# Second norm of three block boundaries from three sums gathered early, odd residual tiles on GpSimd

## What is computed

```python
def rmsnorm(x, g):
    xf = x.astype(jnp.float32)
    y = xf * lax.rsqrt(jnp.mean(xf * xf, axis=-1, keepdims=True) + EPS)
    return (y * g.astype(jnp.float32)).astype(x.dtype)
...
        f = swiglu(rmsnorm(h, ffn1_pre_g[l]), ffn1_w_gate[l], ffn1_w_up[l], ffn1_w_down[l])
        h = h + 0.5 * rmsnorm(f, ffn1_post_g[l])
        m = hybrid_mixer(rmsnorm(h, mix_pre_g[l]), w_in[l], b_gate[l], q_norm_g[l], w_uq[l],
                         kv_norm_g[l], w_ukv[l], w_sb_o[l], w_mla_o[l], w_out[l])
        h = h + rmsnorm(m, mix_post_g[l])
        f = swiglu(rmsnorm(h, ffn2_pre_g[l]), ffn2_w_gate[l], ffn2_w_up[l], ffn2_w_down[l])
        h = h + 0.5 * rmsnorm(f, ffn2_post_g[l])
    return h[:, N_META:]
...
        h = rms_norm(x, norm1_g[l]) * (1.0 + sc1) + sh1
        z = h @ w_in[l]
```

## Time and profile before

| | |
|---|---|
| median of 3 runs | 1902.59 us (1902.04 to 1903.81) |
| the profiled execution's own time | 1902.07 us |
| its span | 1900.3 us |
| mean granted PE clock | 0.986 of full speed |

### The profile page before, as it was taken

How to read it: one execution, slowest core, us unless ns; L and a number is a source line. 1 busy time by engine, 2 the same in 40 slices (tenths; PEclk the granted TensorE clock), 3 DMA queues, 4 the chain that set the end, 5 groups by cost and what they waited for, 6 DMA issues and landing times.

```text
span 1900.3 us, 30514 instructions
## 1 busy us (share of the span) xinstructions
PE 1804.4 (95%) x11032; PEld 1143.7 (60%) x11033; DVE 1024.9 (54%) x1509; ACT 524.7 (28%) x847; POOL 852.6 (45%) x481
## 2 busy tenths in 40 slices
PE   8999998998999999998999999999989999999987
PEld 7999896677899998888633333333333333333332
DVE  6776642345687575658455554454454554444444
ACT  5333443635643345345310110110110110011011
POOL 0000000000000026647178777777777777777774
PEclk9999999989999999899999999999999999999999
DMA  9777452213476643333899999999999999999995
GB/s 350 262 257 262 175 178 89 67 48 111 164 270 251 202 156 136 132 112 133 354 373 419 416 419 416 418 418 417 419 417 408 417 417 418 417 419 417 419 417 221
DMA packets 98894, 560.96 MB, mean 295 GB/s; under 512 B 9008, under 2 KB 11184, under 8 KB 50480
## 3 DMA queue, kind: packets, MB, share of 16 engines
q1 hardware_dynamic: 98688, 560.02, 74.9%
q10 hardware_dynamic: 144, 0.07, 0.0%
HBM read 559.00 MB, written 1.05 MB: 295 GB/s over the span
## 4 chain that ended last, share of the span: by engine, by line
PE 70%; DMA 15%; DVE 7%; ACT 3%; POOL 3%; issue 2%; SPq 0%; POOLq 0%; DVEq 0%; ACTq 0%
PE bank L1193 16%; DMA stage<-w_exp_in 15%; PE bank L665 12%; PE bank L667 11%; PE bank L666 11%; PE bank L1280 8%; POOL ring L1720 2%; DVE cst L1745 2%; PE bank L1204 1%; PE bank L646 1%; PE bank L908 1%; DVE cst L2288 1%; DVE arena L1745 1%; DVE cst L1749 1%; PE bank L1260 1%
## 5 line engine op out<-in xcount | busy, mean ns | idle before, releaser
L1720 POOL COPY ring<-stage 128x2048 f32<-128x2048 f32 x372 | 717.7, 1937 | 249.4 <-DMA stage<-w_exp_in 134.9
L1193 PE MATMUL bank<-ring,arena 128*64 128x512 f32 x2112 | 474.9, 597 | 11.2 <-POOL ring L1720 11.1
L1701 POOL TENSOR_TENSOR w_lo<-ring,w_hi 128x512 fp32r<-128x512 f32 x104 | 134.7, 1329 | 776.4 <-ACT w_hi L1338 776.4
L665 PE MATMUL bank<-x_hi,w_hi 128*128 128x256 f32 (+1 forms) x1336 | 388.1, 291 | 8.8 <-DVE x_lo L1801 4.3
L667 PE MATMUL bank<-x_hi,w_lo 128*128 128x256 f32 (+1 forms) x1336 | 383.8, 287 | 0.0
L666 PE MATMUL bank<-x_lo,w_hi 128*128 128x256 f32 (+1 forms) x1336 | 383.5, 287 | 0.0
L1193 PEld LDWEIGHTS bank<-ring,arena 128*64 128x64 f32 x2112 | 145.3, 137 | 304.4 <-issue 249.5
L665 PEld LDWEIGHTS bank<-x_hi,w_hi 128*128 128x128 f32 x1336 | 257.0, 192 | 20.1 <-issue 11.6
L1765 DVE TENSOR_TENSOR w_lo<-ring,w_hi 128x2048 fp32r<-128x2048 f32 x92 | 210.5, 2289 | 96.8 <-ACT w_hi L1338 94.6
L667 PEld LDWEIGHTS bank<-x_hi,w_lo 128*128 128x128 f32 x1336 | 257.4, 193 | 0.0
L666 PEld LDWEIGHTS bank<-x_lo,w_hi 128*128 128x128 f32 x1336 | 256.4, 192 | 0.1
(11 more groups left out here) (340 smaller groups left out, 1992.8 us busy)
## 6 DMA issues: line engine op xcount, KB each, us to landing
stage<-w_exp_in SPq DMA_DIRECT2D x248, 1024.0 KB, 12.6
stage<-w_exp_out SPq DMA_DIRECT2D x124, 1024.0 KB, 12.8
ring<-stream SPq DMA_DIRECT2D x120, 1024.0 KB, 4.9
arena<-ada SPq DMA_DIRECT2D x48, 512.0 KB, 4.0
ring<-w_exp_in SPq DMA_DIRECT2D x8, 1024.0 KB, 6.8
ring<-w_exp_out SPq DMA_DIRECT2D x4, 1024.0 KB, 11.1
cst<-const_in SPq DMA_DIRECT2D x1, 1584.0 KB, 19.3
arena<-b_exp SPq DMA_DIRECT2D x3, 384.0 KB, 8.5
```

Source lines behind the costliest of these rows:

```text
L665: begin = mm(out_, wh, xh, start=start, stop=False)
L1193: last = mm(bank[2 + gu][pr, :], xT[:, k % 4, k // 4, :], ring[:, k, c0:c0 + 512], start=False, stop=(k == KD - 1), tile_position=pos)
L1701: nc.gpsimd.tensor_tensor(w_lo[:, BUF[p], c:c + REST_COLS], ring[:, p % RING, c:c + REST_COLS], w_hi[:, BUF[p], c:c + REST_COLS].bitcast(f32),
L1720: nc.gpsimd.tensor_copy(ring[:, j, :], stage[:, j % STAGED, :]).then_inc(in_place, 1)
```

## The change

For u = y times the gain, r the reciprocal root of the first norm, and h the old residual, the new residual is h + r u, and its sum of squares is sum(h^2) + 2 r sum(h u) + r^2 sum(u^2). The first sum is kept in `a_sum` from boundary to boundary. The other two are gathered while the last projection runs. ACT evacuates each tile with three activations instead of two: the square of y, u itself (the gain is now applied here), and the square of u (`post_tile`). DVE adds up both sets of squares (`add_post_squares`, two additions a tile instead of one). POOL multiplies u with the old residual and adds up the products of tiles 0 to 6 (`product`); DVE makes the product of tile 7 (`last_product`). PE sums the three over partitions with six matmuls (`boundary_sums`), then twelve idle ones, in place of the two and eight with twenty idle ones. When the first root is there, four small DVE operations give the new sum, and ACT makes the second root from it (`root_of_new`), without the new residual. DVE updates the even residual tiles in between its normed tiles (`boundary`), POOL the odd ones (`update_odd`). The table with Ln and Exp is loaded ahead of the last projection. POOL's first two weight rests stand behind the products of tiles 5 and 6 of the third boundary. The bias, gain and mask preparations on DVE stand behind `last_product` now.

```diff
-            norm_sum_of_two("f1_post", TOK)
-            keep_running(10)
-            norm_sum("mix_pre", KD, TOK)
-            keep_running(10)
+            boundary_sums("f1_post", TOK, sq, sq[:, 6, :])
...
+            def boundary_sums(n, width, squares, added):
+
+                i = BOUNDARIES[n]
+                ones, y, c, b = const("ones"), bank[7][:, 0:width], bank[0][:, 0:width], bank[1][:, 0:width]
+                pe.wait_ge(n_side, AT[n_side][n] + 1)
+                mm(y, ones, squares[:, (KD - 2) % 3, 0:width], start=True, stop=False)
+                pe.wait_ge(c_side, i + 1)
+                mm(c, ones, squares[:, 3 + (KD - 2) % 3, 0:width], start=True, stop=False)
+                pe.wait_ge(n_sq, AT[n_sq][n] + KD)
+                mm(y, ones, squares[:, (KD - 1) % 3, 0:width], start=False, stop=True).then_inc(n_sum, 1)
+                pe.wait_ge(b_side, i + 1)
+                mm(b, ones, added, start=True, stop=False)
+                pe.wait_ge(OUT[n][0], OUT[n][1] + KD)
+                mm(c, ones, squares[:, 3 + (KD - 1) % 3, 0:width], start=False, stop=True).then_inc(more_sums, 1)
+                pe.wait_ge(b_last, i + 1)
+                mm(b, ones, last_prod[:, 0:width], start=False, stop=True).then_inc(more_sums, 1)
+                keep_running(12)
...
+            def post_tile(i, m, b, gain, to, squares):
+
+                if m >= 3:
+                    act.wait_ge(n_add, i * 10 + 2 * (m - 2))
+                A(squares[:, m % 3, 0:b.shape[1]], b, ACT.Square).then_inc(n_sq, 1)
+                A(to, b, ACT.Copy, scale=gain).then_inc(n_u, 1)
+                return A(squares[:, 3 + m % 3, 0:b.shape[1]], b, ACT.Square, scale=gain)
...
+                use("natural_log_exp_and_others")
+                half = half_f2 if f else half_f1
                 m = 0
...
-            root("f1_post", TOK, D, "eps1")
-            squares("mix_pre", KD, lambda m: res[:, m, :], updated["f1"])
-            root("mix_pre", TOK, D, "eps1")
+            root("f1_post", TOK, D, "eps1", to=r1)
+            root_of_new(0, TOK, "eps1")
...
+            def product(i, m, u, r, prod, added):
+
+                pool.wait_ge(n_u, i * KD + m + 1)
+                if m == 0:
+                    step(gt(added, u, r, ALU.mult))
+                    return
+                pool.wait_ge(pool_steps, steps[0])
+                step(gt(prod, u, r, ALU.mult))
+                pool.wait_ge(pool_steps, steps[0])
+                last = gt(added, added, prod, ALU.add)
...
+            def update_odd(n, u, into, width):
+
+                pool.wait_ge(n_rs, AT[n_rs][n] + 1)
+                for m in range(1, KD, 2):
+                    if m == KD - 1:
+                        pool.wait_ge(b_last, BOUNDARIES[n] + 1)
+                    step(gt(u(m), u(m), r1[:, 0:width], ALU.mult))
+                    pool.wait_ge(pool_steps, steps[0])
+                    gt(into(m), into(m), u(m), ALU.add).then_inc(odd_updated, 1)
...
+            for m in range(KD - 1):
+                product(2, m, nrm[:, m, 0:SEQ], real(res[:, m, :]), sq[:, 7, 0:SEQ], sq[:, 6, 0:SEQ])
+                if m >= KD - 3:
+                    rest(POOL_PIECES[m - KD + 3])
+            update_odd("f2_post", lambda m: nrm[:, m, 0:SEQ], lambda m: real(res[:, m, :]), SEQ)
+            for p in POOL_PIECES[2:]:
+                rest(p)
...
+            def last_product(n, u, r):
+
+                dve.wait_ge(n_u, (BOUNDARIES[n] + 1) * KD)
+                tt(last_prod[:, 0:u.shape[1]], u, r, ALU.mult).then_inc(b_last, 1)
+
+            def boundary(n, pre, width, u, into, gain, dst, then):
+
+                i = BOUNDARIES[n]
+                t, ss = s2[:, 0:width], a_sum[:, TOK - width:TOK]
                 dve.wait_ge(n_rs, AT[n_rs][n] + 1)
...
+                dve.wait_ge(more_sums, 2 * i + 1)
+                link(tt(t, bank[0][:, 0:width], r1[:, 0:width], ALU.mult))
+                dve.wait_ge(more_sums, 2 * i + 2)
+                link(stt(t, bank[1][:, 0:width], 2.0, t, ALU.mult, ALU.add))
+                link(tt(t, t, r1[:, 0:width], ALU.mult))
+                tt(ss, ss, t, ALU.add).then_inc(new_sum, 1)
+
+                def update(m):
+                    link(tt(u(m), u(m), r1[:, 0:width], ALU.mult))
+                    tt(into(m), into(m), u(m), ALU.add).then_inc(even_updated, 1)
+
+                update(0)
+                dve.wait_ge(n_rs, AT[n_rs][pre] + 1)
                 for m in range(KD):
...
+                    if m % 2:
+                        dve.wait_ge(odd_updated, 4 * i + m // 2 + 1)
+                    else:
+                        if m:
+                            update(m)
+                        dve.wait_ge(even_updated, 4 * i + m // 2 + 1)
+                    stt(dst(m), into(m), gain(m), rstd[:, 0:width], ALU.mult, ALU.mult).then_inc(n_out, 1)
                     if m:
...
             ffn(1, FFN2_AT, SEQ)
+            last_product("f2_post", nrm[:, KD - 1, 0:SEQ], real(res[:, KD - 1, :]))
             dve.wait_ge(ada_used, ADA_TILES)
             link(tt(mod, mod, vec("b_ada", 0, 48), ALU.add))
```

141 lines of the change are left out of this document (82 added, 59 removed).

## The result

The changed kernel takes **1908.91 us** in the median of 19 runs (1903.37 to 1915.53), beside 1902.35 us for the kernel before (19 runs, 1898.95 to 1904.83). The ratio on record is **1.0031 [1.0023, 1.0039]** (the medians alone give 1.0034): it is slower by 0.3%, where 0.4% faster was forecast. In this document numbers in brackets behind a ratio are its 95% interval. The profiled execution took 1913.35 us, its span is 1911.6, and the mean granted clock 0.978 (before: 0.986). It lies 4.4 us above the median, so its parts are read with that in mind.

A forecast was written before the change was run, and what follows sets the result against it. PE's waits at three boundaries were taken to bound the dense part, DMA the experts' stretch. Gains 3.8 + 2.4 + 1.5 = 7.7 us from 1902.07 gave 1894.4, as median 1894.9; range 1888.5 to 1901.

The forecast's parts named there:

- The chain at the first boundary: First boundary: 6.25 us gained if nothing gets in the way, less 2.5 for POOL beside DVE, leaving 3.8.
- over 0.9 was to be a sign of being wrong: POOL's operations of 272 columns, forecast at about 0.7 us, would show the prediction wrong if they took over 0.9.
- The excess x: Extra time of a DVE operation with SBUF inputs beside a POOL one: 0.35 us, forecast range 0.2 to 0.48.
- Rival (a): DVE is hardly held, since POOL's operations wait for their own semaphores: gain 11 to 15 us; chance 0.13.
- rival (b): Strict lock between DVE and POOL, excess 0.7, limited to POOL's eight operations: gain about 1 us, 1901.5; chance 0.12.
- 17.0 - 27x: Gain in us of the three boundaries together, x being the excess of a DVE operation beside POOL.
- Rival (e): Low clock when projections start: 1.4 us lost at each of three boundaries, gain 3.5, time 1899; chance 0.04.
- Second boundary: Root to projection 9.9 us less 4.7, then less 2.5 for POOL and 0.3 for DVE's rest: gain 2.4.
- that cover: POOL's products and DVE's second additions run under PE's down projection, with microseconds of room for a tile of 22 products.
- Third boundary: x_hi of tile 7 comes at about 723.2 instead of 724.73, the rigid chain behind it: gain 1.5 us.
- Table load ahead of w_out: ACT's table load falls where DVE sets the pace, so it is covered; uncovered it costs 1.28 us once.
- (d): The boundaries' gain is lost in the experts' stretch because the DMA engines are full there: 1902; chance 0.04.

## Why the prediction was wrong

**The chain at the first boundary: right in kind.** First root 0.6 us earlier on the chain (2.52 us behind the first sum, before 3.14), forecast 0.5; the new sum in four operations; PSUM operations spared (0.44); POOL's first two operations took 0.76, forecast 0.7, and the six behind them 0.83 to 0.96 (over 0.9 was to be a sign of being wrong). The excess x was 0.49, not 0.35, just past the forecast's upper edge of 0.48, and it hit seven operations where the text counts nine. Rival (a) is dead; rival (b), a strict lock with 0.7, was too strict here: 0.93 us in the mean, while 0.44 + 0.76 is 1.20. A DVE operation that starts midway would only wait for the rest of POOL's, but even so: the one at 222.24 starts 0.07 us behind POOL's at 222.17 and ends 0.29 behind its end, less than its own 0.44. With x = 0.49 the prediction's own formula, 17.0 - 27x, gives 3.8 us, so this term alone makes it 1898.8 and not 1908.9. With the clock at full the boundary is worth 3.1 us at the mixer's weight rest.

**The clock: a term left out of the sum, the first step that failed.** Rival (e) had the mechanism, priced at 1.4 us for each boundary, 4.2 in all, and 0.04 of the chance; the sum has it at nothing. It put the wait ahead of a projection at some 2 us, and the waits were 4.54, 2.73 and 7.39. The clock fell at all three boundaries. More idle matmuls alone gave 5.1 us back and brought the mean clock from 0.981 to 0.987, where it stands in the kernel before. By place the price was wrong: at the first boundary the half clock cost 2.6 us in the profile after (sum to weight rest 64.09, against 61.53 at full clock) and 1.4 in four other profiles with the same code there (62.9); at the third it cost nothing that the profiles show (POOL's weight rest 29.46 us behind the first sum with it and without it); and the second ran its sums at half clock, which (e) didn't foresee. Over the 19 runs of the changed kernel the time goes with the mean clock by 1.26 us per 0.001, from 1903.5 us at 0.986 to 1914.4 at 0.978; between 0.987 before and 0.981 after that is about 7.5 us, more than the loss. This is a correlation and not a proof, and three things speak for care: fewer idle matmuls cost nothing; the clock held at the third boundary moved nothing there; and most of the half-clock time of the dense part after lies in the two mixers (30.7 and 28.7 us, the third boundary's in the second), most of it far from any boundary. Of one profile for each kernel one can't say that the changed kernel meets it oftener: the first mixer has 17.1 to 30.7 us of it in the profiles with 12 idle matmuls, and 17.1 to 30.7 in those whose waits are short, the kernel before among them. So a clock term of about 5 us is shown by the experiment, and what ties the rest to the boundaries stays open. By the Trainium skill, "TensorE: Matmul & The Clock Gate", Part 1, the clock follows how busy the array has lately been; the trace agrees at the boundaries, where each fall stands behind the start of a wait.

**Second boundary: 2.4 us of gain forecast, 2.0 of loss found; the second step that failed.** The text saw one microsecond ahead of the sums (rest later, one addition, POOL's product between), and it was 3.07. It said of POOL's products that they ran under PE's projection with room; that holds in the FFNs, where a tile has 22 products, but the sums there still came 0.54 us later at the first. In w_out a tile has eight and DVE is the pace: the failed step is that cover. The two kernels that leave out parts of the sums show it: without POOL 2.33 of the 3.07 us come back. The price was readable: DVE's rests of 2.29 us stand nearly end to end in that stretch. Behind the sums the new form gave 1.02 us up to the third boundary in the profile after, and between +1.0 and -0.8 in the other profiles that have it with GpSimd's updates.

**Third boundary: 1.5 forecast, 1.3 lost by POOL's weight rest; the third step that failed.** The preparations ended 4.5 us behind the root and not 3, and POOL's second weight rest ended at 716.43, 4.6 us behind the first sum and not 3.1 (706.9 less 703.83), so that its updates began 2.1 us behind the root. x_hi of tile 7 came at 734.04, 22.2 us behind the first sum against 20.9 before. Moving the preparations gave 4.4 us in the medians.

**Table load ahead of w_out and experts' stretch.** The load is hidden, as said: with idle matmuls added the two rests around it are 8.06 us apart, before 8.05. (They are 9.55 apart in the profile after, and also in one of a kernel without this load: there the clock stood at half.) The experts' stretch kept its length within 2.4 us, so (d) is small; that it can grow by 21 from 0.09 us nobody had written down.

**What it would have taken.** The kernel with the preparations first, the second boundary left alone, and 24 idle matmuls takes 1898.0 us: of the 7.7 us forecast for three boundaries, 4.8 are there with two, once DVE's order, the gathering in w_out and the filler are mended. The three single edits gave 4.4, 3.1 and 5.1 us, 12.6 in sum, and all together 10.9, so they overlap.

## What to carry to other kernels

Count a boundary to the end of the tiles that stream through it, not to the moment the matmul engine starts: of a start 2.3 us earlier 1.2 were left at one boundary, and at another the same edit was 2.3 us slower at the end. When a chain gets shorter but its wait is filled with less, look at the clock behind the wait and try the filler at a new size: 12 idle matmuls were 5 us too few, and 36 or 22 at the third boundary made no difference to the end of its tiles. Work gathered "under" a stage is free only where the engine that must gather it has slack in that stage; read it stage by stage. And where a stretch that nobody touched differs by 6 us between two profiles, look at its clock before the difference is put down to the change.

## What the runs showed of the hardware

- DVE with two SBUF inputs beside POOL, 128x272: 0.88 to 0.99 us in place of 0.44, POOL 0.95 in place of 0.76; with a PSUM input 0.44. For 512 columns beside a copy of 1.89 us: 0.69 where it starts 0.02 us ahead of the copy, 1.51 or 2.37 where it starts 0.92 or 0.08 behind the copy's start.
- A copy 0.09 us late in one of twelve places of a loop changed a stretch of 960 us by 21 to 24, and went away when 24 unrelated fills were put ahead of the loop.
- The same stretch of 200 us, instruction for instruction, took 200.6, 202.1, 205.2 or 206.6 us, with TensorE at half clock in it for 17.1, 20.5, 27.3 or 30.7 us.
- After one and the same wait of 1.9 us the clock was 0.57 in one profile and 1.00 in another.
